# Extra TensorE products, whose results nobody reads, placed in seven waits of a two-block transformer kernel

## What is computed

```python
def first_block(x, ...):                      # depth 2
    x = x + mlstm_mixer(rmsnorm(x), ...)      # 4 heads, two directions, chunks of 128
    x = x + swiglu(rmsnorm(x), ...)           # 1024 -> 2 x 2816 -> 1024
    x = x + window_attn_mixer(rmsnorm(x), positions, ...)   # 16 query heads, 4 key heads, rope, window 128, sink
    x = x + swiglu(rmsnorm(x), ...)
    return rmsnorm(x)

def second_block(x, meta_tokens, ...):        # 16 meta rows ahead of the 256
    u = rmsnorm_2(concat(meta_tokens, x))
    proj = u @ w_in                           # split into 11 parts
    o_mla = causal_block_attention(q_m, k_m, v_mla, MLA_SCALE)      # 16 heads
    o_fox = causal_block_attention(fq, fk, fv, FOX_SCALE, cum)      # 16 heads, with forget gates
    mixed = (sigmoid(gate_a) * y_mla + sigmoid(gate_b) * y_fox) @ w_out
    return x + rmsnorm_2(mixed)
```

## Time and profile before

| | |
|---|---|
| median of 3 runs | 1028.2 us (1025.29 to 1029.03) |
| the profiled execution's own time | 1030.92 us |
| its span, first to last instruction | 1028.9 us |
| mean granted TensorE clock | 0.984 of full speed |
| PE busy | 974.7 us, 95% of the span |
| PE weight loads busy | 816.8 us, 79% |
| DVE busy | 589.2 us, 57% |
| ACT busy | 480.5 us, 47% |
| chain that ended last, by engine | PE 78%, DVE 9%, ACT 5%, DMA 3%, issue 2% |

### The profile page before, as it was taken

How to read it: one execution, slowest core, us unless ns; L and a number is a source line. 1 busy time by engine, 2 the same in 40 slices (tenths; PEclk the granted TensorE clock), 3 DMA queues, 4 the chain that set the end, 5 groups by cost and what they waited for, 6 DMA issues and landing times.

```text
span 1028.9 us, 14249 instructions
## 1 busy us (share of the span) xinstructions
PE 974.7 (95%) x5267; PEld 816.8 (79%) x5267; DVE 589.2 (57%) x1096; ACT 480.5 (47%) x762; POOL 24.0 (2%) x39
## 2 busy tenths in 40 slices
PE   6999799899999989999999999989899999999996
PEld 6876587688888889887888888878898888888875
DVE  4854757553546577457454545764764456555665
ACT  5554446344444346546353535564433344444442
POOL 0002200000000000000000000000000000000000
PEclk9999999899999999899999999999999999999999
DMA  5651245445454522235535364312432234333441
GB/s 207 242 200 46 82 166 182 161 148 219 147 220 149 199 104 83 82 121 205 223 144 229 138 229 163 141 42 103 172 110 82 81 124 149 125 123 124 143 164 41
DMA packets 25349, 149.49 MB, mean 145 GB/s; under 512 B 2992, under 2 KB 3120, under 8 KB 11088
## 3 DMA queue, kind: packets, MB, share of 16 engines
q1 hardware_dynamic: 24624, 146.39, 39.0%
q0 software_dynamic: 672, 2.38, 0.7%
HBM read 147.71 MB, written 1.05 MB: 145 GB/s over the span
## 4 chain that ended last, share of the span: by engine, by line
PE 78%; DVE 9%; ACT 5%; DMA 3%; issue 2%; DVEq 2%; SPq 0%; ACTq 0%
PE bank L427 22%; PE bank L428 21%; PE bank L429 21%; DMA w_raw<-w_main_dram 3%; DVE w_lo L1633 2%; PE bank L486 2%; DVE w_lo L1547 1%; ACT w_hi L1135 1%; PE bank L812 1%; ACT w_hi L1080 1%; PE bank L932 1%; DVEq L1960 1%; PE bank L673 1%; PE bank L799 1%; PE bank L947 1%
## 5 line engine op out<-in xcount | busy, mean ns | idle before, releaser
L427 PE MATMUL bank<-w_hi,x_hi 128*128 128x512 f32 (+2 forms) x664 | 267.3, 403 | 1.8 <-DVE ffn_nat L1856 1.3
L428 PE MATMUL bank<-w_lo,x_hi 128*128 128x512 f32 (+2 forms) x664 | 260.1, 392 | 0.0
L429 PE MATMUL bank<-w_hi,x_lo 128*128 128x512 f32 (+2 forms) x664 | 258.5, 389 | 0.0
L1547 DVE TENSOR_TENSOR w_lo<-w_raw,w_hi 128x2048 fp32r<-128x2048 f32 x56 | 126.8, 2289 | 48.1 <-ACT w_hi L1080 47.9
L427 PEld LDWEIGHTS bank<-w_hi,x_hi 128*128 128x128 f32 x664 | 125.3, 189 | 31.3 <-issue 4.3
L429 PEld LDWEIGHTS bank<-w_hi,x_lo 128*128 128x128 f32 x664 | 124.7, 188 | 27.9
L428 PEld LDWEIGHTS bank<-w_lo,x_hi 128*128 128x128 f32 x664 | 125.0, 188 | 23.1
L1633 DVE TENSOR_TENSOR w_lo<-w_raw,w_hi 128x2048 fp32r<-128x2048 f32 x46 | 105.2, 2290 | 50.9 <-ACT w_hi L1135 50.8
L1080 ACT ACTIVATE w_hi<-w_raw 128x2048 fp32r<-128x2048 f32 x58 | 109.6, 1912 | 43.0 <-DMA w_raw<-w_main_dram 36.3
L1135 ACT ACTIVATE w_hi<-w_raw 128x2048 fp32r<-128x2048 f32 x46 | 87.3, 1907 | 16.9 <-PE bank L429 12.3
L1856 DVE SCALAR_TENSOR_TENSOR ffn_nat<-bank,stat,ffn_nat 128x256 f32<-128x256 f32 x44 | 21.1, 482 | 124.7 <-ACT ffn_nat L1266 124.6
(11 more groups left out here) (326 smaller groups left out, 1525.7 us busy)
## 6 DMA issues: line engine op xcount, KB each, us to landing
w_raw<-w_main_dram SPq DMA_DIRECT2D x111, 1024.0 KB, 4.9
s_raw<-w_side_dram SPq DMA_DIRECT2D x51, 512.0 KB, 4.1
h<-x_dram SPq DMA_DIRECT2D x2, 512.0 KB, 4.7
w_raw<-w_main_dram SPq DMA_DIRECT2D x2, 512.0 KB, 7.5
arena<-rows_dram POOLq DMA_DIRECT2D x2, 512.0 KB, 3.9
out_dram<-arena SPq DMA_DIRECT2D x1, 512.0 KB, 2.6
out_dram<-arena SPq DMA_DIRECT2D x2, 256.0 KB, 2.1
arena<-c_l_dram POOLq DMA_DIRECT2D x1, 384.0 KB, 6.0
```

What stands on the lines that cost most here:

```text
L427: pe.matmul(out, ah, bh, start=first, stop=False)
L428: pe.matmul(out, ah, bl, start=False, stop=False)
L429: return pe.matmul(out, al, bh, start=False, stop=last)
L1547: dve.tensor_tensor(w_lo[:, slot, 4 * g:4 * g + 4, :], w_raw[:, g, :, :], w_hi[:, slot, 4 * g:4 * g + 4, :], ALU.subtract).then_inc(w_lo_o ...
```

## The change

A helper `idle_products(n, to, operand)` issues `n` matmuls of 128 columns, each of an operand with itself, into the first 128 columns of a PSUM bank that is free at that point. Their results are never read. It is called in seven places: 52 products ahead of the wait for the first loads; 28 after the turns of tiles 0 and 1 of the mixer's output and 32 ahead of the turn of its tile 4, after `st_wait` of tile 2; 24 ahead of `a_turn(0)` and 20 behind it, ahead of `a_scores(1)`; 28 in group 2 of the first attention ahead of `a_turn(10)`; and 30 in the last loop between the scores of heads 1 and 2. The operand is `zero_r`, and `x_hi` in the last of them. Otherwise the order on each engine is as before.

```diff
+            def idle_products(n, to, operand):
+
+                for _ in range(n):
+                    pe.matmul(to[:, 0:P], operand, operand, start=True, stop=True)
+
+            pe.wait_ge(zero_ok, 1)
+            idle_products(52, bank[7], zero_r)
             pe.wait_ge(in_landed, 32)
...
-            streamed("m_out", xn, {0: lambda: pe.wait_ge(xn_ready, 1), 4: lambda: pe.wait_ge(xn_ready, 2)}, [m_out_tiles])
+            def second_pairs_ready():
+                idle_products(32, bank[5], zero_r)
+                pe.wait_ge(xn_ready, 2)
+
+            pe.wait_ge(xn_ready, 1)
+            to_stationary("m_out", xn, None, 0, ks=range(2))
+            idle_products(28, bank[5], zero_r)
+            streamed("m_out", xn, {4: second_pairs_ready}, [m_out_tiles], ahead=False)
...
             for j in range(NG):
                 n = NG * j
+                if j == 0:
+                    idle_products(24, bank[5], zero_r)
                 a_turn(n)
+                if j == 0:
+                    idle_products(20, bank[7], zero_r)
...
                 for i in range(1, NG):
+                    if (j, i) == (2, 2):
+                        evacuated(("aq", 3))
+                        idle_products(28, acc[USE[("aq", 3)] % 2], zero_r)
                     a_turn(n + i)
...
             for n in range(2 * NH):
                 if n == NH - 1:
                     pe.wait_ge(cum_ok, 1)
+                if n == 0:
+                    idle_products(30, bank[7], x_hi[:, 0, M:M + P])
                 if n + 2 < NH:
                     head_scores(n + 2)
```

## The result

The changed kernel took a median of 1038.46 us (4 runs, 1037.58 to 1041.42). The ratio is 1.0103 [1.0074, 1.0132]: slower by 1.0%. Forecast were 1026.1 us and a range to 1031.5, so the prediction was wrong, in sign and in range.

A forecast was written before the change was run, and what follows sets the result against it. PE, busy for 95% of the span, was taken to set the end, with half-speed stretches behind its waits. Terms -2.5 + 1.9 - 0.1 - 1.3 - 0.1 = -2.1 us took the median from 1028.2 to 1026.1 us; range 1021.8 to 1031.5.

The forecast's parts named there:

- What one product costs: All batches: a 128-column product takes 0.109 us at full speed and 0.218 at half speed.
- how long steady work takes to bring the full clock back: All batches: 4.1 to 6.1 us of steady work, read from four low stretches of the profile before.
- Start: 52 products ahead of the first loads: first real product 0.3 us late, full clock gains 2.86; -2.5 us (0 to -2.9).
- products of zeros do not hold or bring the clock: Rival: all 52 start products at half speed, 11.3 us, first weight product 3.3 late; total 1037.6 us; chance 0.05.
- the 28: First attention, ahead of `a_turn(10)`: later turns at full speed, -1.3 us (-2.0 to +1.1, the latter had the clock held before).
- I take it as lasting: Start: the 2.5 us gain was expected to persist, since later weight loads are issued earlier by as much.
- First batch of the mixer's output: 28 products behind the first turns: tiles 0 and 1 come 1.05 us late, hidden by a later wait; cost 0.
- Batch of 32: Mixer's output, behind tile 2's wait: costs its full 3.49 us, full clock gives back 1.60; +1.9 us (to +3.5).
- so I expect no fall: Mixer's output: the clock stays full through the 32, so three tiles take 4.83 us instead of 6.43.
- First attention: 24 and 20 products around `a_turn(0)`: `a_scores(1)` 1.6 us late, removed low stretch gives back 1.7; -0.1 us (to +1.6).
- Last loop: 30 products ahead of head 2's scores: 1.3 us late, removed low stretch gives it back; -0.1 us (-0.4 to +1.3).
- Before, the low stretches were only partly there: Rival: other executions before lack some of the five low stretches, so products only delay; about 1029.5 us; chance 0.17.

The follow-up runs named there:

- fit_ffn: fit_wide with 18 start products instead of 20 and 22 of 512 columns in a first feed-forward wait, its first loop turn written out; 1020.61 us, 0.993 to before.
- start_alone: Kernel before plus only the 52 products of 128 columns at the start; 1033.61 us, ratio 1.0038.
- start_ones: Kernel before plus only the 52 start products, of a tile of ones instead of zeros; 1032.09 us in one run.
- start_wide: Kernel before plus 24 products of zeros with 512 columns at the start; 1028.16 us, ratio 0.9997.
- mout2_wide: Kernel before plus 15 products of 512 columns at the place of the mixer's output batch of 32; 1030.01 us in one run.
- same_places_wide: Changed kernel with its seven batches at the same places and full-speed lengths, made of 512-column products; 1031.42 us, ratio 1.0038 to the kernel before.
- mout2_alone: Kernel before plus only the 32 products of 128 columns at the mixer's output; 1034.58 us, ratio 1.0065.
- five_left: Changed kernel without the 52 start products and the 32 at the mixer's output; 1031.84 us, ratio 1.0015 to the kernel before.
- fit_narrow: fit_wide with every batch after the start made of 128-column products of the same length; 1025.1 us, ratio 0.9983 to the kernel before.
- fit_wide: Kernel before plus 512-column batches placed in waits and cut to their length, two of them in mLSTM head 0; 1023.39 us, ratio 0.9952.

## Why the prediction was wrong, step by step

**What bounds the kernel: right.** PE's list sets the end. Low clock behind waits is a real loss: from before to fit_ffn the time at half speed falls from 28.7 to 8.4 us, of which half is 10.2, and the median falls by 7.8.

**What one product costs: half right.** 0.109 was forecast at full speed, and 24 took 2.63 us, 0.110 each; 0.218 at half speed was 11.35 / 52. The step that failed is the next sentence of that part, "how long steady work takes to bring the full clock back", 4.1 to 6.1 us, taken from stretches of real work and applied to products of 128 columns. In three of those stretches PE worked mostly at products of 144 to 512 columns. The fourth, from 417.01 to 422.80, held transposes of 128 and products of 64 columns, and the clock came back there too; so it is not shown that narrow work can't bring it back anywhere. But fifty-two 128-column products in a row did not bring the clock back in 11.35 us, 24 of 512 columns did (start_alone, start_ones, start_wide). The Trainium skill ("TensorE: Matmul & The Clock Gate", section "Why this matters for your kernels") advises to keep TensorE continuously busy, and to warm it up with matmuls, to have its full clock; by that the 52 would have been enough, and for 128 columns the trace does not agree.

**Start: -2.5 forecast, +3.25 at the mixer's output measured.** This is the larger failed step. 2.21 of the 3.25 are the start's, read at mLSTM head 0, so the step was wrong by 4.7 us; the other 1.04 come from low stretches that the change does not touch. The path was read rightly, since with wide products the gain came, 1.9 of 2.5 us (start_wide); the return of the clock within the 52 was wrong. "I take it as lasting" is not borne out either: start_wide had lost its lead by 120 us. I had the very number in the rival "products of zeros do not hold or bring the clock" (11.3 us of products, first weight product 3.3 late; measured 11.35 and 3.56) and gave it 0.05. Its mechanism as I put it was wrong too: zeros are not the reason, since ones behave alike. That its total, 1037.6 us, lies within 1 us of the measured 1038.46 is luck: it has scores 1.6 later, of which 0.13 was left at `a_turn(1)`, the 28 at +1.1, which gave -1.3, and the batch of 32 at 3.5, which cost 5.1.

**First batch of the mixer's output: right.** Tile 2's turn is 127.27 against 122.94, 4.33 late, which is 1.08 more than the start's 3.25 (forecast 1.05), and the 32 begin 3.14 late (131.70 against 128.56), so it was hidden.

**Batch of 32: +1.9 forecast, +5.1 measured** (8.39 less 3.25). The place was read rightly: the batch stands behind the wait and not in it. The term "so I expect no fall" failed, by 3.2 us: the batch cost 5.13 us up to the turn of tile 4 (131.70 to 136.83) instead of 3.49, and the three tiles behind it took 6.55 (to 143.38) instead of 4.83; it began 0.1 less late than the turns ahead. The wait ahead of it shrank from 2.21 to 1.03 us, and the clock still fell; with 15 wide products behind the full 2.12 us it did not (mout2_wide), nor behind 1.14 us (same_places_wide), and there +1.8 and +1.9 were measured. That this holds in every execution is not shown by two profiles.

**First attention: right.** `a_scores(1)` was 1.74 later than `a_scores(0)` was (9.72 less 7.98, forecast 1.6), and by `a_turn(1)` it was down to 0.13 (forecast -0.1). The 28 gave -1.3 from `a_scores(3)` (418.72 against 410.35, 8.37 late) to the turn at 431.31 (against 424.24, 7.07 late), forecast -1.3. **Last loop:** -0.3 (7.01 late ahead of it, 702.23 against 695.22; 6.68 some 10 us behind), forecast -0.1. Here 20 to 30 narrow products, begun at full speed, kept it.

**The sum.** Between the forecast for the profiled execution (-2.1) and the measured +6.7 lie 8.8 us. The two failed steps hold 4.7 + 3.2 = 7.9 of them. Low stretches outside the seven places hold +1.0 (ahead of the mixer's output) and -0.4 (first feed-forward layer), which the forecast had counted at 0. The rest is 0.3.

**Before, the low stretches were only partly there: right, and given too little.** The forecast counted the removed stretches as if each execution had them. Over its 68 runs the kernel before was at half speed for 28.7 us, its profiled run (0.984) for 33. The profiles of the kernels that leave a place as it was show how the stretches vary. Near the first attention's scores of group 1 three of six have one (before, start_alone, start_ones). At the last loop it is three of six again (before, start_ones, start_wide). At `a_turn(11)` all six have one, but it is 6.8 us long in two (before, start_alone) and 3.4 in four. So the -1.3 of the 28 came true against a profile that had the long one. Even with wide products in the change's places, which keep the clock in the profile, the kernel ended 3.0 us above before, where the forecast of -2.1 stood for just that behaviour. That is a miss of 5 us which is hidden in the profile-to-profile sum: there, forecast and measurement share the same high start.

**Closure by single parts.** start_alone (+0.38%), mout2_alone (+0.65%) and five_left (+0.15%, which is not told from 0) give +1.18%, against 1.03% [0.74, 1.32] measured for the whole.

**Open.** Whether it is the width of a product or its share of weight loads that decides at the start; why the same wait is followed by a low clock in one execution and not in another; why the 32 let the clock fall after a wait of 1.03 us while 24 and 20 did not after theirs; why transposes and 64-column products were enough at 417 to 423 us of the profile before, and 52 products of 128 columns were not at the start; and whether narrow products are worse in short fitted batches too (fit_narrow against fit_wide, 1.7 us with overlapping intervals).

## What to carry to other kernels

Unread products can hold TensorE's clock through a wait, but test the shape first, at the start of the kernel, where it shows at once in the pitch. Make them 512 columns wide (in fitted waits the narrow ones were not told from them, at the start they failed), place each batch inside the wait, ahead of the instruction that waits, and make it no longer than the wait: what stands beyond it is paid in full on an engine that runs its list in order. And judge the gain against the clocks of many runs of the kernel before, since one profile shows one draw of its low stretches.

## What the runs showed of the hardware

- At the start the granted clock reads 1.00 over 1.10 to 12.40 us while the products are 0.218 apart, twice the 0.110 of the same product at 389 us. Half speed at the start must be read from the pitch.
- 52 products of 128 columns with their weight loads, zeros or ones, did not bring full speed back in 11.35 us of unbroken work, in three profiles of three; 24 products of 512 columns, 8.27 us, did (start_wide).
- Without any change at the start its length varies: the scores of mLSTM head 0 came at 67.54 to 69.15 us in five profiles.
- The spread of the kernel before is mostly that of its clock: in its 6 runs with a mean of 0.981 the median is 1032.84 us, in the 17 with 0.989 or more it is 1024.32.
